# Half of the output projection streamed beside the state scan, and one program from the scan to the value projection

## The reference

```python
h = rms_norm(x, norm_mix_g[l])
u = h @ w_in[l]
y_ssd  = ssd_mixer(u[..., :SSD_IN], ...)       # state scan, 16 heads of 64
y_rwkv = rwkv7_mixer(u[..., SSD_IN:], ...)     # time mixing, 16 heads of 64
x = x + jnp.concatenate([y_ssd, y_rwkv], axis=-1) @ w_out[l]
h = rms_norm(x, norm_x_g[l])
m = rms_norm(mem, norm_mem_g[l])
x = x + memory_cross_attention(h, m, wq, wk, wv, wo)
```

## Time and profile before

| | |
|---|---|
| median of 3 runs | 3005.47 us (3005.35 to 3005.65) |
| the profiled execution's own time | 3006.09 us |
| its span, first to last instruction | 3004.3 us |
| PE busy | 2846.4 us, 95% |
| DVE busy | 1836.8 us, 61% |
| ACT busy | 1240.2 us, 41% |
| POOL busy | 501.2 us, 17% |
| mean granted TensorE clock | 0.975 |
| read from HBM | 503.12 MB, 170 GB/s over the span |

### The profile page before, as it was taken

The page is one execution under the profiler, slowest core; times in us unless marked ns, Lnnn a source line. Parts: engine busy times, 40 slices in busy tenths (PEclk is TensorE's granted clock), DMA queues, the critical chain, the costliest instruction groups (busy, mean ns, idle before and its releaser), DMA issues. The chain is left out here.

```text
span 3004.3 us, 60723 instructions
## 1 busy us (share of the span) xinstructions
PE 2846.4 (95%) x24198; PEld 2790.8 (93%) x24198; DVE 1836.8 (61%) x2108; ACT 1240.2 (41%) x1489; POOL 501.2 (17%) x573
## 2 busy tenths in 40 slices
PE   8999587699999899999999999999999999999997
PEld 8998586599999899999999999998999999999997
DVE  6657744566444565555555576799667655765664
ACT  5344211344333454344444453633454443444443
POOL 0000120248000223920064130000121000010011
PEclk9999788899999999999999999999999999999999
DMA  6553000355552556566565755645555555566564
GB/s 233 195 190 119 15 1 1 120 173 184 177 192 80 172 196 193 193 227 204 190 197 188 234 196 175 207 173 173 171 196 194 194 194 187 192 197 196 186 196 141
DMA packets 138264, 513.93 MB, mean 171 GB/s; under 512 B 15344, under 2 KB 15600, under 8 KB 136816
## 3 DMA queue, kind: packets, MB, share of 16 engines
q1 hardware_dynamic: 138096, 511.58, 51.5%
HBM read 503.12 MB, written 8.40 MB: 170 GB/s over the span
## 5 line engine op out<-in xcount | busy, mean ns | idle before, releaser
L665 PE MATMUL acc<-a,hi 128*128 128x256 f32 x5504 | 1526.0, 277 | 24.9 <-DVE lo L471 21.7
L666 PE MATMUL acc<-a,hi 128*128 128x256 f32 x5504 | 1520.3, 276 | 0.0
L667 PE MATMUL acc<-a,lo 128*128 128x256 f32 x5504 | 1520.2, 276 | 0.0
L471 DVE TENSOR_TENSOR lo<-raw,hi 128x1024 fp32r<-128x1024 f32 x704 | 913.2, 1315 | 676.3 <-ACT hi L370 674.4
L665 PEld LDWEIGHTS acc<-a,hi 128*128 128x128 f32 x5504 | 1034.0, 188 | 29.5 <-issue 23.7
L666 PEld LDWEIGHTS acc<-a,hi 128*128 128x128 f32 x5504 | 1034.1, 188 | 0.8 <-issue 0.5
L667 PEld LDWEIGHTS acc<-a,lo 128*128 128x128 f32 x5504 | 1034.1, 188 | 0.0
L370 ACT ACTIVATE hi<-raw 128x1024 fp32r<-128x1024 f32 x704 | 733.6, 1057 | 642.7 <-PE acc L667 619.4
L617 POOL TENSOR_TENSOR a<-th,a 128x512 f32 (+1 forms) x80 | 119.5, 1494 | 1377.8 <-ACT a L426 1377.7
L471 DVE TENSOR_TENSOR lo_x<-raw_x,hi_x 128x1024 fp32r<-128x1024 f32 x128 | 180.3, 1419 | 162.6 <-ACT hi_x L370 162.4
L665 PE MATMUL acc<-a,hi_x 128*128 128x256 f32 x768 | 216.1, 281 | 30.7 <-DVE lo_x L471 30.5
(11 more groups left out here) (493 smaller groups left out, 2926.3 us busy)
## 6 DMA issues: line engine op xcount, KB each, us to landing
raw<-in_ffn SPq DMA_DIRECT2D x256, 512.0 KB, 4.1
raw_in<-in_w_in SPq DMA_DIRECT2D x96, 512.0 KB, 3.9
raw<-in_w_in SPq DMA_DIRECT2D x92, 512.0 KB, 3.4
raw<-in_up_gate SPq DMA_DIRECT2D x88, 512.0 KB, 4.3
raw<-in_up_val SPq DMA_DIRECT2D x88, 512.0 KB, 4.2
raw<-in_down SPq DMA_DIRECT2D x88, 512.0 KB, 4.2
raw_x<-in_w_out SPq DMA_DIRECT2D x32, 512.0 KB, 4.3
raw_x<-in_wq SPq DMA_DIRECT2D x32, 512.0 KB, 3.4
```

Source lines behind the costliest of these rows:

```text
L471: eng.tensor_tensor(self.lo[:, slot, :], self.raw[:, slot, :], self.hi[:, slot, :].bitcast(F32), ALU.subtract).then_inc(self.s_lo, 1)
L665: eng.matmul(out, self.hi[:, slot, cols], a[:, 0, :], start=opens, stop=False)
L666: eng.matmul(out, self.hi[:, slot, cols], a[:, 1, :], start=False, stop=False)
L667: ins = eng.matmul(out, self.lo[:, slot, cols], a[:, 0, :], start=False, stop=closes)
```

## The change

1. `w_out` becomes two arrays, `w_out_s` (the scan's 1024 rows) and `w_out_r` (the time mixing's), and two phases of 8 units of 2 chunks: `w_out_r` of kind `acc` (adds to `x` only), `w_out_s` of kind `gained`.
2. `ssd` becomes the class `ChunkedScan`. Its instructions on PE are cut into 14 pieces that are issued ahead of the 16 chunks of `w_out_r` (`tensor(eng, n)`, called by `Stream.unit` before chunk n); on ACT and DVE the chunk's `hi` and `lo` are written into the scan's own list. The stream has PSUM banks 0 and 1 of `acc`, so the scan's transposes and outputs use banks 2 and 3, and its inputs are transposed chunk by chunk.
3. Scan, `w_out_s`, `wq`, `wk` and `wv` are one Block. The Block that clears `tb` is gone.
4. The memory norm is cut into pieces in the query stream: the squares, the gained copy and the low part go to ACT and DVE; POOL keeps the adding of the squares, now after `w_out_s`. The memory is loaded once the scan has ended.
5. Kind `resid` is gone; `gained` writes the high part on ACT straight from `x` and the low part on DVE (`gained_low`), for `w_out_s`, `wo` and `w_out_2`. POOL's subtraction of a unit (L617) goes there.

```diff
-SPLITS = ("resid", "relu2", "val", "glu_val", "br_ssm")
+SPLITS = ("relu2", "val", "glu_val", "br_ssm")
...
-        if kind in ("resid", "gained", "sumsq"):
...
+        if kind in ("gained", "sumsq"):
             at_least(eng, self.s_pool, v + b["pool"])
+        if kind == "gained":
+            out = pair(ph.out, v, ph.t0)
             for t in range(2):
-                ins = eng.activation(self.th[:, s, t, :], tile(self.x, v * 2 + t), ACT.Copy,
+                ins = eng.activation(out[:, t, 0, :], tile(self.x, v * 2 + t), ACT.Copy,
                                      scale=self.gain(ph.g, v * 2 + t))
-            ins.then_inc(self.s_alink, 1)
-            eng.activation(self.tq[:], pair(self.x, v), ACT.Square)
-            eng.wait_ge(self.s_alink, v + (b["alink"] + 1))
+            ins.then_inc(self.s_ghigh, 1)
...
+        def tensor(eng, n):
+
+            if n == 0:
...
+                turn_inputs(eng, 0)
+            elif n == 2:
                 eng.wait_ge(dar, 1)
                 eng.matmul(s.work[:, 3, 0:NH], s.const("lower"), da[:, 0, :], start=True, stop=True).then_inc(decs, 1)
+            elif n == 3:
                 eng.wait_ge(xdr, 2)
                 eng.wait_ge(bck, 1)
+                turn_inputs(eng, 1)
...
+            elif 4 <= n < 12:
+                segment(eng, n - 4)
+                if n > 4:
+                    ssd_y(eng, n - 5)
+            elif n == 12:
+                ssd_y(eng, 7)
+            elif n == 14:
...
+            for it in range(8):
+                c, q, gi = it // 4, it % 4, it % 2
+                eng.wait_ge(elr, it + 1)
+                at_least(eng, yr, it - 1)
+                eng.tensor_tensor(mm[:, gi], el[:, gi], over(cbm[:, q // 2, c, :], 4), ALU.mult).then_inc(mmr, 1)
+                if it + 2 < 8:
+                    mask(it + 2)
+                chunk(it + 5)
+                eng.wait_ge(yr, it + 1)
...
+            for n in range(13, 16):
+                chunk(n)
...
-                w_out = s.phase("w_out", "w_out", 8, 4, 2, s.a0, "resid", out=a1, g="norm_x_g")
-                q = s.phase("wq", "wq", 8, 4, 2, a1, "scaled", out=qx, after=w_out, sum_after=True)
-                memory = MemoryNorm(dram, s, vx, kx, w_out, semaphores(nc, rg))
+                ws = s.phase("w_out_s", "w_out_s", 8, 2, 4, s.a0, "gained", out=a1, g="norm_x_g",
+                             ready=lambda eng: eng.wait_ge(scan.low, 2))
+                q = s.phase("wq", "wq", 8, 4, 8, a1, "scaled", out=qx, after=ws, sum_after=True)
+                memory = MemoryNorm(dram, s, vx, kx, scan, sem)
+                k = s.phase("wk", "wk", 8, 4, 2, s.a0, "plain", out=kx, ready=lambda eng: eng.wait_ge(memory.low, 2))
+                v = s.phase("wv", "wv", 8, 4, 2, s.a0, "tok", out=vx)
+                phs = [ws, q, k, v]
...
                     def _(eng):
-                        s.pe(eng, [w_out, q], aside=memory.pe)
-                k = s.phase("wk", "wk", 8, 4, 2, s.a0, "plain", out=kx)
-                v = s.phase("wv", "wv", 8, 4, 2, s.a0, "tok", out=vx)
-                stream_block(nc, s, [k, v])
+                        for n in range(wr.units):
+                            s.unit(eng, wr, n, n, beside=scan.tensor)
+                        s.pe(eng, phs, beside=(q, memory.pe))
```

More of the change, by code:

```diff
@@ L1503, in sp @@
     def sp(self, eng, q):
+        if q == 0:
+            eng.wait_ge(self.scan.low, 2)
         n = KT * T // 4
-        eng.dma_start(self.flat[:, q * n:(q + 1) * n], self.dram["mem"][:, q * n:(q + 1) * n]).then_inc(self.loaded, 16)
-    def pe(self, eng):
-        eng.wait_ge(self.squared, 1)
-        eng.matmul(self.s.work[:, 0, 0:T], self.s.const("ones"), self.sq[:, 0, :], start=True,
-                   stop=True).then_inc(self.summed, 1)
-    def act(self, eng):
-        eng.wait_ge(self.summed, 1)
-        eng.activation(self.root, self.s.work[:, 0, 0:T], ACT.Sqrt, scale=1.0 / D,
-                       bias=self.s.eps[:, 0:1]).then_inc(self.rooted, 1)
@@ new lines, in pe, with act @@
+    def pe(self, eng, v):
+        if v == 4:
+            eng.wait_ge(self.added, 1)
+            eng.matmul(self.s.work[:, 0, 0:T], self.s.const("ones"), self.sq[:, 0, :], start=True,
+                       stop=True).then_inc(self.summed, 1)
+    def act(self, eng, v):
+        s = self.s
+        if v in (0, 1):
+            for q in (2 * v, 2 * v + 1):
+                eng.wait_ge(self.loaded[q], 16)
+                eng.activation(self.sq[:, 4 * q:4 * q + 4, :], self.mem[:, 4 * q:4 * q + 4, :],
+                               ACT.Square).then_inc(self.squared, 1)
+        if v == 4:
+            eng.wait_ge(self.summed, 1)
+            eng.activation(self.root, s.work[:, 0, 0:T], ACT.Sqrt, scale=1.0 / D, bias=s.eps[:, 0:1]).then_inc(self.rooted, 1)
+        if v in (6, 7):
+            for kt in range(KT // 2 * (v - 6), KT // 2 * (v - 5)):
+                if kt % 4 == 0:
+                    eng.wait_ge(self.scaled, kt // 4 + 1)
+                ins = eng.activation(s.a0[:, kt, 0, :], self.mem[:, kt, :], ACT.Copy, scale=s.par("norm_mem_g", kt))
+            ins.then_inc(self.high, 1)
@@ L1642, in _, with attentions @@
             s.pe(eng, phs)
-def attentions(nc, dram, s):
+def attentions(nc, dram, s, u):
     with ExitStack() as st:
+        sem = semaphores(nc, st)
+        wr = s.phase("w_out_r", "w_out_r", 8, 2, 2, s.a0[:, 8:16], "acc")
+        with ExitStack() as early:
+            place = alloc(nc, early, "u_place", [P, U_TILES, T])
+            scan = ChunkedScan(nc, early, s, u, sem, wr)
         a1 = alloc(nc, st, "a1", [P, KT, 2, T], F32R)
@@ L2373, in feed_forwards @@
         a2 = alloc(nc, st, "a2", [P, KT, 2, T], F32R)
-        fo = s.phase("wo", "wo", 8, 4, 2, a1, "resid", out=s.a0, g="norm_ffn_g")
+        fo = s.phase("wo", "wo", 8, 4, 2, a1, "gained", out=s.a0, g="norm_ffn_g")
         ffn = [fo]
@@ L2405, in feed_forwards @@
         bs = s.phase("br_ssm", "br_ssm", 8, 1, 8, s.a0[:, 4:8], "br_ssm", out=a2, src=ub, g0=KT, after=g2, lead=True)
-        wo = s.phase("w_out_2", "w_out_2", 8, 4, 2, a2, "resid", out=s.a0, g="ffn2_g", after=bs)
+        wo = s.phase("w_out_2", "w_out_2", 8, 4, 2, a2, "gained", out=s.a0, g="ffn2_g", after=bs)
         phs = [ba, g1, g2, bb, bs, wo]
@@ L2577, in mixers @@
         rwkv(nc, dram, s, u, low, lw)
-        ssd(nc, s, u)
+    return u
 def tiled(a):
```

489 lines of the change are left out of this document (239 added, 250 removed).

## The result

| | before | after |
|---|---|---|
| median | 3005.41 us (3005.34 to 3005.65, 4 runs) | 2967.59 us (2967.12 to 2973.26, 4 runs) |
| ratio, 95% interval | | 0.9879 (0.9867 to 0.9890) |
| profiled execution | 3006.1 us, span 3004.3 | 2967.9 us, span 2966.1 |
| PE busy | 2846.4 us | 2842.9 us |
| POOL busy | 501.2 us | 383.0 us |

What follows compares the result with a forecast made beforehand. PE, busy 95% of the span, was taken as the bound; only its standing, off-stream work or half clock could yield. 37.9 us (scan to `wv`) plus 1.4 (`gained`) made 39.3, so 2966 us, range 2957 to 2985.

Steps and rivals of the forecast that it cites:

- Start of the joint program: Between time mixing and scan: giving back one more semaphore set moves the start from 516.84 to 517.6; chunk 0 at 523.9.
- Interleaved part: Scan beside `w_out_r`, through chunk 13: PE's list sums to 61.5 us without waits; chunk 13 ends at 586.6.
- fourteen handovers: Between engines in the interleaved scan and stream: 1.2 us in all, with ends of nothing and 7 us.
- Scan's tail: Sums of squares to `w_out_s`: PE done at 595.6, stands 4.8 us, goes on at 600.4 with a 2.6 us half-clock start.
- Joins: Standing and half clock to be saved: 9.0 us inside `w_out`, 9.3 us between `wq` and `wk`.
- Memory norm at nothing: Memory norm's pieces on ACT and DVE in the query stream cost PE 0; ends 0 and 2 us.
- POOL's adding at nothing: POOL's adding of the memory's squares, now in the second and third query unit, costs 0; other end 5 us.
- `gained`: At the joins `wo` to `ffn1` and `w_out_2` to `gate`, PE no longer waits for POOL's subtraction: gain 1.4 us.
- no chain got in PE's way: Rival, scan steps: interleaved lists obstruct each other, up to 2.2 us in each of eight steps, 17.6, giving 2984; chance 0.15.
- the memory was not late: Rival, join between `wq` and `wk`: late memory norm brings back up to 9.3 us, giving 2975; chance 0.10.
- the clock had 0.91 in the stretch: Rival, 523.9 to 595.6: scan and stream run at half clock, 70 us more, giving 3036; chance 0.05.
- the overlap is worth 13 us: Rival, scan beside stream: each chunk lengthens the scan by its own time, leaving some 22 us gain, 2983; chance 0.08.

Runs made afterwards that it cites:

- e1: Changed kernel with `wk` and `wv` again a separate program; median 2976.80 us, stretch (scan's first matmul to cross attention's first) 406.2 against 395.7 us.
- e3: Changed kernel with the memory's squares back on POOL, they and their adding ahead of POOL's units of `w_out_s`; median 2980.57 us, stretch 410.5 us.
- e8: Changed kernel with `wo` and `w_out_2` back to kind `resid`, `w_out_s` staying `gained`; median 2968.14 us, stretch 396.3 us.
- e6: Changed kernel with chunk 13's low part written on DVE ahead of the gate products, during the wait for the last output; median 2966.64 us, stretch 393.2 us.
- e7: Changed kernel with 32 idle matmuls on PE behind chunk 15, in the gap ahead of `w_out_s`; median 2964.33 us, stretch 392.8 us.
- e9: Changed kernel with e5's edit and DVE's sum of stream unit 6 moved behind the scan's first reciprocal and scaling; median 2961.22 us, stretch 393.6 us.
- e11: Changed kernel with scan steps one chunk earlier, sums of squares ahead of chunk 12, and e9's moved sum; median 2962.11 us, stretch 393.6 us.
- e4: Changed kernel with the memory's squares back on POOL, behind its units of `w_out_s`, right ahead of the adding; median 2963.49 us, stretch 395.3 us.
- e5: Changed kernel with the scan's sums of squares on PE ahead of chunk 13 instead of chunk 14; median 2964.41 us, stretch 395.9 us.
- e10: Changed kernel with e9's edits and the 32 idle matmuls of e7; median 2964.16 us, stretch 393.4 us.
- e12: e11 with ACT writing the high parts of chunks 13 and 14 ahead of the scan's squares; median 2963.45 us, stretch 389.0 us.
- e2: Changed kernel with PE running the whole scan first, then the sixteen `w_out_r` chunks; median 2980.61 us, stretch 408.9 us.

## Why the prediction was right

- *Start of the joint program.* The idle time of PE ahead of it grew from 9.51 to 10.32 us: 0.8, as taken. That the start was still 0.9 us later than 517.6 is the time mixing ahead of it, which the change does not touch.
- *Interleaved part.* Counted from PE's first scan instruction, chunk 0 was put at 6.3 us and came at 5.8; chunk 13's end at 69.0, and the sums behind it began at 587.37 - 518.47 = 68.9. The list of 61.5 us came out at 61.7, partly by luck. Chunk 0 took 4.2 us instead of 2.7, since it began at half clock, for which the list had no place; the product for the state took 1.9 instead of 3.0, and a step in the second chunk of tokens 5.7 instead of 5.9. With a late rise of the clock, as in e1, e3 and e8, the same list would have been 1.3 to 1.5 us longer. The 1.2 us that were taken for fourteen handovers are one wait instead: 1.29 for chunk 13's low part, which on DVE stands behind 2.36 us of gate products. e6 shows that it can be had back. I had not looked for what stands ahead of that chunk.
- *Scan's tail.* PE was to be done at 595.6 - 517.6 = 78.0 and was at 78.0; `w_out_s` was to start at 82.8 and did at 81.8, after 3.8 us instead of 4.8. From the sums' start to the scan's last low part it took 11.6 us, not 12.4. The half-clock start was put at 2.6 because the gap lay nearer to the known ones than to nothing: 2.75 by the rows, 2.5 by e7. That the clock falls here was right, its price depends on the execution (e6, e8, e9 and e11 lose 1.4 to 1.7).
- *Joins.* 9.3 us for the one ahead of `wk`: 10.0 to 10.5 in e1. The one in `w_out` was put at 9.0 and not undone alone; e3 shows its chain, a wait for POOL's place, not its size.
- *Memory norm at nothing.* PE has no wait in the query stream and none ahead of `wk`, though DVE stands for ACT's copies in the last unit, and behind it the low part of the next chunk:

```profile
718.30 3.25 DVE L1566 SCALAR_TENSOR_TENSOR a<-vx,prm,a 128x256 fp32r<-128x256 f32 x8 [1.97 <-ACT a L1550]
```

- *POOL's adding at nothing.* Beside POOL's additions from 661.32 DVE needs 10.27 us for four low parts, twice the usual 4 x 1.23 = 4.9:

```profile
661.32 10.21 POOL L1575 TENSOR_TENSOR kx<-kx 128x2048 f32<-128x2048 f32 x3 [7.35 <-ACT kx L1541]
...
664.02 10.27 DVE L463 TENSOR_TENSOR lo_x<-raw_x,hi_x 128x1024 fp32r<-128x1024 f32 x4
```

  That agrees with the Trainium skill (SBUF — State Buffer, section "SBUF: two separate sides"), by which they exclude each other, but the 1 us on PE that I had worked out by that rule did not come: PE does not stand in the query stream. In e4 POOL worked there for 13.9 us more, and again nothing.
- *`gained`.* 1.4 us were forecast. The waits for POOL are gone (0.67 us each in e8), but the part behind the stretch is only 0.5 us shorter, because the clock fell at `w_out_2`'s start in this execution, for which the sum had no place. Where it held (e5, e6, e9, e11) that part is 1.3 to 1.8 us shorter than the 2052.4 of before; but e8, which has `resid` as before, was itself 0.4 shorter. With the 0.8 to 1.3 of e8 the term was about right. One execution does not resolve it: where the clock fell, this part took from 2051.2 (e7) to 2054.5 us (e3, e10).

The sum of 39.3 us stands against 38.2 measured: 39.35 in the stretch, where 37.9 and the 0.8 of the later start are 38.7 and 0.4 came from the join behind `wv`, which the sum left out (PE idle for 1.05 us there instead of 1.49); 0.5 behind it for 1.4; 1.6 given back ahead of it for 0.8. The rivals: no chain got in PE's way but once for 1.3 us, the memory was not late, the clock had 0.91 in the stretch that would have decided it and 1.00 from 528 to 598, and the overlap is worth 13 us.

## What to carry to other kernels

When two programs are laid into one list, count not only whether each engine has time in a step but what stands directly ahead of the instruction that the busiest engine waits for next: here three single instructions on DVE and ACT (a gate product, a sum onto `x`, a high part) held a tail of 12 us, and moving the sums alone gave nothing. A gap of 2.4 to 5.7 us on TensorE cost 1.4 to 2.6 us more behind it in clock here (rest of 312.8 to 314.0 us against 311.4), so it is worth closing wholly (e12) or filling with matmuls that nobody waits for (e7), rather than halving it (e11). And compare kernels from a common instruction, with an eye on the clock at both ends: several edits here were worth less than the spread of equal code.

## What the hardware showed besides

**The same code ahead of the change took different times.** The scan's first matmul came between 513.3 us (e10) and 519.3 us (e6) with nothing changed before it, which is as much as most experiments here move. PE's busy time in the time mixing goes with it; e6 first, then e10:

```profile
280.00:510.00 230.00, 176.35 (x1266) 0.83 0.02 5
```

```profile
280.00:510.00 230.00, 170.67 (x1255) 0.85 0.02 5
```

Nearly the same work (the windows are fixed, so a few instructions differ), 5.7 us more of PE's time, and a granted clock of 0.83 against 0.85. It fits that e4, equal to the changed kernel within 0.5 us in the stretch, has a median 4 us lower: its scan began 4.5 us earlier in the profiled execution.

**A gap of the same length had the clock fall in some executions and not in others.** Ahead of `w_out_2` PE stands 1.8 to 1.9 us in every kernel. In the changed kernel, after 1.85 us, and in the one before, after 1.86:

```profile
2142.00:2144.00 2.00, 2.00 (x11) 0.50 0.88 285
```

```profile
2180.00:2182.00 2.00, 2.00 (x20) 1.00 0.80 260
```

It fell in the changed kernel, e1, e2, e3, e4, e7, e10 and e12, and held in the one before, e5, e6, e8, e9 and e11; the kind of the phase, which e8 changes, has no part that these runs could separate. A gap of 1.6 us inside the cross attention did the same: behind it the clock fell in e3, e9, e10 and e11 alone. The Trainium skill (TensorE: Matmul & The Clock Gate, section "Part 1: The HAM clock gate (the "warmup" mystery)") says that the window in which a block of the chip watches the engine is free-running, so that the same kernel can see its clock change at different points; the runs agree in that they differ, and can't show more. What decides it in one execution stays open. The price was about 1.6 us. When the clock comes up again behind the scan's start differs in the same way, as the second table of the experiments shows.
